# One hybrid decoder layer step on one core: first weight half in front of the tokens, and the first products in front of the mean of squares

## What is computed

```python
def rms_norm(x, g):
    xf = x.astype(jnp.float32)
    y = xf * lax.rsqrt(jnp.mean(xf * xf, -1, keepdims=True) + EPS)
    return (y * g.astype(jnp.float32)).astype(x.dtype)

def mixer_in(x, pos, g_pre, w_in):
    z = rms_norm(x, g_pre) @ w_in
    u = z[..., :CONV_CH] * jax.nn.sigmoid(z[..., CONV_CH:c0])
    ...   # q, k, v and gates are further columns of z
```

## Time and profile before

| | |
|---|---|
| time, median of 3 runs | 779.73 us (779.62 to 781.24) |
| time of the profiled execution | 778.18 us |
| its span in the profile | 775.7 us |
| mean granted clock of PE | 0.988 |
| busy: PE, DVE, ACT, POOL | 745.4, 465.4, 249.2, 316.0 us |

### The profile page before, as it was taken

The page is one execution under the profiler, slowest core; times in us unless marked ns, Lnnn a source line. Parts: engine busy times, 40 slices in busy tenths (PEclk is TensorE's granted clock), DMA queues, the critical chain, the costliest instruction groups (busy, mean ns, idle before and its releaser), DMA issues.

```text
span 775.7 us, 14868 instructions
## 1 busy us (share of the span) xinstructions
PE 745.4 (96%) x6211; PEld 698.6 (90%) x6211; DVE 465.4 (60%) x683; ACT 249.2 (32%) x447; POOL 316.0 (41%) x130
## 2 busy tenths in 40 slices
PE   8999999999998798999999999999999999999993
PEld 7999999987897655589999999999999999999992
DVE  5999978788767477833296333800025767733236
ACT  6422532243556577653343212200002122110021
POOL 1100000023301300002607576876775876776774
PEclk9999999999999799999999999999999999999997
DMA  9532420357624931101314133153223133123103
GB/s 359 181 108 99 138 96 18 133 177 220 229 96 129 288 10 55 56 1 55 109 57 163 55 109 108 56 216 108 63 100 109 56 108 108 58 106 108 55 1 110
DMA packets 25041, 85.50 MB, mean 110 GB/s; under 512 B 7216, under 2 KB 12896, under 8 KB 17760
## 3 DMA queue, kind: packets, MB, share of 16 engines
q1 hardware_dynamic: 17760, 62.13, 24.6%
q0 software_dynamic: 3456, 16.78, 6.6%
q10 hardware_dynamic: 3776, 5.89, 2.0%
HBM read 80.51 MB, written 8.47 MB: 115 GB/s over the span
## 4 chain that ended last, share of the span: by engine, by line
PE 89%; DVE 6%; ACT 3%; issue 1%; DMA 1%; SPq 0%; DVEq 0%; ACTq 0%
PE PA L1527 27%; PE PB L1527 27%; PE PB L1850 5%; PE PB L1538 2%; PE PA L1538 2%; PE PR L1952 2%; PE PR L1702 1%; PE PS L1987 1%; PE PS L1723 1%; PE PB L1978 1%; PE PA L1978 1%; DMA wraw<-wblk_dram 1%; DVE smx L1334 1%; PE PA L1687 1%; PE PR L1629 1%
## 5 line engine op out<-in xcount | busy, mean ns | idle before, releaser
L434 POOL TENSOR_TENSOR wH<-wraw,zero 128x2048 fp32r<-128x2048 f32 x29 | 105.3, 3631 | 110.6 <-PE PB L1527 87.1
L437 POOL TENSOR_TENSOR wL<-wraw,wH 128x2048 fp32r<-128x2048 f32 x29 | 139.5, 4811 | 2.3
L1429 DVE TENSOR_TENSOR hL<-h,hH 128x520 f32 (+1 forms) x32 | 64.6, 2022 | 47.1 <-ACT hH L883 47.1
L881 ACT ACTIVATE h<-rl 128x520 f32<-128x520 f32 x32 | 20.4, 638 | 209.3 <-DVE rl L1424 208.6
L999 DVE SCALAR_TENSOR_TENSOR yC<-uP,vec,yC 128x512 f32<-128x512 f32 (+1 forms) x135 | 84.2, 682 | 0.1
L1527 PE MATMUL PA<-hL,wH 128*128 128x260 f32 x240 | 67.7, 282 | 0.0
L1527 PE MATMUL PB<-hL,wH 128*128 128x260 f32 x240 | 67.7, 282 | 0.0
L1527 PE MATMUL PA<-hH,wL 128*128 128x260 f32 x240 | 67.7, 282 | 0.0
L1527 PE MATMUL PA<-hH,wH 128*128 128x260 f32 x240 | 67.7, 282 | 0.0
L1527 PE MATMUL PB<-hH,wL 128*128 128x260 f32 x240 | 67.7, 282 | 0.0
L1527 PE MATMUL PB<-hH,wH 128*128 128x260 f32 x240 | 67.7, 282 | 0.0
(11 more groups left out here) (515 smaller groups left out, 2317.8 us busy)
## 6 DMA issues: line engine op xcount, KB each, us to landing
wraw<-wblk_dram SPq DMA_DIRECT2D x46, 1024.0 KB, 4.8
xT<-x_fm_dram SPq DMA_DIRECT2D x4, 520.0 KB, 5.0
xT<-x_fm_dram SPq DMA_DIRECT2D x1, 2080.0 KB, 12.6
y_fm_dram<-xT SPq DMA_DIRECT2D x8, 260.0 KB
rkw<-cwk_dram SPq DMA_DIRECT2D x8, 256.0 KB, 2.8
s_win_dram<-cwk_dram ACTq DMA_DIRECT2D x1, 2044.0 KB
s_win_dram<-cwv_dram ACTq DMA_DIRECT2D x1, 2044.0 KB
p_rows_dram<-ktok ACTq DMA_DIRECT2D x4, 256.0 KB, 3.3
```

Source lines behind the costliest of these rows:

```text
L434: pool.tensor_tensor(wH[1 - s][:, :], wraw[s][:, :], zero[:, :].broadcast_to([P, BW]), ALU.add)\
L437: pool.tensor_tensor(wL[1 - s][:, :], wraw[s][:, :], wH[1 - s][:, :].bitcast(F32), ALU.subtract)\
L881: act.activation(h2[c % 2][:, :], rl[c % 2][:, :], ACT.Square).then_inc(s_h2, 1)
L1429: dve.tensor_tensor(lo, h2[c % 2][:, :], hi.bitcast(F32), ALU.subtract).then_inc(s_hl, 1)
```

## The change

SP issues the vectors first, then the first half of the first block (k = 0 to 3) with a semaphore of its own, the first two token tiles, the second half of the block, and then the other token tiles. DVE applies the gains to its four parts ahead of the pair adds. PE makes the first block's products for k = 0 and 1, then the sums of pairs 0 and 1, the products for k = 2, the sums of pairs 2 and 3, and then the products for k = 3 to 7. ACT's list stays as it is: the root still stands ahead of its gains. Nothing else differs; the same instructions run, with one transfer more.

```diff
@@ sync
-            for i in range(4):
+            sp.dma_start(vec[:, :], A["vecs"]).then_inc(s_vec, 16)
+            sp.dma_start(wraw[0][:, 0:BW // 2], A_wblk[B_IN][:, 0:BW // 2]).then_inc(s_w0, 16)
+            load_x(0)
+            sp.dma_start(wraw[0][:, BW // 2:BW], A_wblk[B_IN][:, BW // 2:BW]).then_inc(s_raw[0], 16)
+            for i in range(1, 4):
                 load_x(i)
-            sp.dma_start(vec[:, :], A["vecs"]).then_inc(s_vec, 16)
-            sp.dma_start(wraw[0][:, :], A_wblk[B_IN]).then_inc(s_raw[0], 16)
             sp.dma_start(wraw[1][:, :], A_wblk[B_IN + 1]).then_inc(s_raw[1], 16)
@@ vector
+            dve.wait_ge(s_vec, 16)
+            dve.wait_ge(s_w0, 16)
+            for k in range(4):
+                dve.tensor_scalar(first_w[:, k * 2 * P:(k + 1) * 2 * P], wraw[0][:, k * 2 * P:(k + 1) * 2 * P],
+                                  vec[:, V_GPRE + k:V_GPRE + k + 1], None, ALU.mult).then_inc(s_gwd, 1)
             for k in range(0, KT, 2):
                 dve.wait_ge(s_sq0, k + 2)
                 dve.tensor_tensor(psq[k][:, :], psq[k][:, :], psq[k + 1][:, :], ALU.add).then_inc(s_sqp, 1)
-            dve.wait_ge(s_vec, 16)
-            dve.wait_ge(s_raw[0], 16)
-            for k in range(4):
-                dve.tensor_scalar(first_w[:, k * 2 * P:(k + 1) * 2 * P], wraw[0][:, k * 2 * P:(k + 1) * 2 * P],
-                                  vec[:, V_GPRE + k:V_GPRE + k + 1], None, ALU.mult).then_inc(s_gwd, 1)
             rinv(1, 1)
@@ tensor
-            for k in range(0, KT, 2):
-                pe.wait_ge(s_sqp, k // 2 + 1)
+
+            def mean_pair(p):
+                pe.wait_ge(s_sqp, p + 1)
                 for hf in range(2):
-                    mm = pe.matmul(PB[:, hf, 0:HT], ones[:, 0, :], psq[k][:, hf * HT:(hf + 1) * HT],
-                                   start=(k == 0), stop=(k == KT - 2))
-            mm.then_inc(s_st, 1)
+                    mm = pe.matmul(PB[:, hf, 0:HT], ones[:, 0, :], psq[2 * p][:, hf * HT:(hf + 1) * HT],
+                                   start=(p == 0), stop=(p == KT // 2 - 1))
+                if p == KT // 2 - 1:
+                    mm.then_inc(s_st, 1)
@@ tensor, in the loop over k of the first block's products
                     if k == KT - 1:
                         mm.then_inc(s_grp, 1)
+                for p in {1: (0, 1), 2: (2, 3)}.get(k, ()):
+                    mean_pair(p)
             pe.wait_ge(s_split, SPLITS(B_IN + 1))
             pe.wait_ge(s_std, 1)
             first_groups((B_IN + 1) % 2, 0)
```

More of the change, by code:

```diff
@@ L305, in hymba_step @@
         s_sm = sem("att_small")
+        s_w0 = sem("first_weights_half_loaded")
         s_tv, s_ta, s_tp = sem("tail_dve"), sem("tail_act"), sem("tail_pe")
```

## The result

The changed kernel is slower: 786.26 us median (784.79 to 788.4, 6 runs) against 779.67 us (777.52 to 781.24, 6 runs) for the kernel before in the same session. The ratio is 1.0092, 95% interval 1.0076 to 1.0109, that is +7.2 us (5.9 to 8.5). The forecast was +4.4. The direction and the mechanism were right, the size was too small: the ratio on 779.73 us gives 786.9, just above the range's end of 786.8.

What follows compares the result with a forecast made beforehand. PE, 89% of the chain, was taken to bound the kernel; 2.75 us of later second block plus 1.7 us of low clock made +4.4 us, so 784.1 us, range 781.3 to 786.8.

Steps and rivals of the forecast that it cites:

- the mechanism: At the start: products ahead of pair sums delay the mean's chain, PE idles for the second block's `wL`, the clock falls.
- The idle time: Before the second block: PE done at 24.1 us waits for `wL` until 28.4, some 4.2 us.
- the slack of 1.24 us: Second block's `wL`: the mean's chain could come 1.24 us later before PE, taking the block at 25.67, would wait.
- The 1.6 us to be won on the products: First block on PE: all products through at 24.1 us instead of 25.67, 1.6 us won but inside the idle time.
- the transfers: First loads: half block lands at 4.95 us, tokens 0 and 1 at 6.25, second half at 7.5.
- The fixed part: Transfers at the start: 2.4 us of each transfer's time is fixed, apart from its size.
- right behind its 11 first matmuls: PE's start: products begin at about 6.4 us instead of 11.76, the first matmuls ending at 6.06.
- The second clock fall: PE's clock falls near 28 us in the `wL` wait; 3.4 us of work at half speed loses 1.7 us.
- 4.0 as planned: The mean's chain: `s_st`, which the root follows, comes at 15.55 us instead of 11.53, 4.0 us later.
- The clock stays up: Rival: the stall before the second block is there but the clock doesn't fall; +3.1 us, 782.8 us, chance 0.27.
- The change doesn't do what it says: Rival: half block, tokens and second half interleave, tokens land near 7.5 us; about +5.5 us, 785; no separate chance.
- absorbed: Rival: a later PE wait for a transfer takes up the shift; about 780 us, no change, chance 0.07.

Runs made afterwards that it cites:

- e_contig: The changed kernel with the first block laid out in memory as two halves, each with its 4096-byte rows contiguous; ratio to the kernel before 1.0061.
- e_wlfirst: The changed kernel with VectorE making the second block's `wL` in front of the first tile's normalization instead of the sixth; ratio to the kernel before 1.0114.
- e_warm: The changed kernel with 22 instead of 11 matmuls on the ones matrix at the start; ratio to the kernel before 1.0095.
- e_warmfill: The changed kernel with 22 ones-matrix matmuls at the start and 18 more before the wait for the second block's `wL`; ratio to the kernel before 1.0071.
- e_fit: The changed kernel with three token transfers first, reordered pair sums and earlier `wL`s, three convolution steps put off, halves at the old pitch; ratio to the kernel before 1.0057.
- e_oldloads: The changed kernel with the old order of transfers: four token transfers, vectors, then the block in two halves; ratio to the kernel before 1.0150.
- e_whole: The changed kernel with the first block in one transfer of 8192 bytes a row, right behind the vectors; ratio to the kernel before 1.0093.

## Why the prediction was wrong in size

**Right: the mechanism.** The root behind the products, everything on VectorE behind the root, TensorE idle for the second block's `wL`, and the clock falling in that gap: all are in the chain after. The idle time was predicted as 4.2 us and is 4.07; the slack of 1.24 us as well (the `wL` 6.7 later, TensorE 5.4 later). The 1.6 us to be won on the products were not won in the change: they end at 26.99, 1.3 later than before. In e_contig they end at 24.48, 1.2 earlier, and that vanishes in the idle time of 4.08, as predicted.

**The step that failed: the transfers.** "the half block can't start before 1.3 and lands at 1.3 + 2.4 + 1.25 = 4.95; tokens 0 and 1 at 6.25." They landed at 6.2 and 7.43. I took the half block's 1.25 us from a transfer of whole rows of 8192 bytes. e_contig gives the half block contiguous rows and lands at 5.35 and 6.5, with the root at 15.76 for my 15.55 and the second block at 28.56 for my 28.4: with this one term put right, the sum of the prediction holds to 0.2 us up to the stall. Of the 1.2 us by which the half block was late, 0.85 is what the place of its rows makes (6.2 against 5.35), and 0.4 is there with contiguous rows too. The rate that I used is not wrong for every half row: the second half moved at it. I had bounded the landing by 0.5 us upwards, from the issue alone; the row rate of a form that the trace doesn't show was no part of the bound, and should have been. The fixed part was rather too small than too large: the 2.0 us of the Trainium skill (DMA: Bandwidth & Descriptors, "Anatomy of one DMA"), a section on transfers that the general engine issues, would have put the half block 0.4 us earlier still, and e_contig has it 0.4 later than forecast.

**What hung on it, and was left out: the first clock fall.** I had PE start "right behind its 11 first matmuls, which end at 6.06". They ended at 5.34 in this execution and the tokens came at 7.43; the gap of 2.19 us was followed by a clock of 0.50, and the two first tiles took 5.43 us instead of 3.5, all of it in front of the pair sums. In the root's 2.7 us beyond the forecast these are 1.2 of landing and 1.9 of clock, less 0.4: the 0.1 of waiting for the second pair, and 0.3 of the last pair sum, which took 0.88 right behind other matmuls and not the forecast's 1.15. The gap wasn't all of the landing's making: with first matmuls that end at 6.06 it would have been 1.5. In e_wlfirst a gap of 1.21 went with first products as slow, so how long a gap is needed stays open; that an unbroken PE has none of it is what e_warm and e_warmfill show. I had seen that 2.21 us of waiting at 249.63 left the clock at 1.00 and never asked the question at the start.

**The second clock fall** was forecast at 1.7 us; it took 1.4 in the change (the second block 13.4 us long instead of 11.9), 2.4 in e_contig. Its length is 3.4 us in one run and 6.8 in another, so 1.7 was a middle value of something that moves by itself, and that it came near is in part luck. The second fall, behind 4.07 us, agrees with the Trainium skill (TensorE: Matmul & The Clock Gate, "Why this matters for your kernels"), which warns of idle gaps between bursts of matmuls. The first came behind a gap of 2.19 us, shorter than those it warns of; there the measurement decides.

**The rivals.** "The clock stays up" is what e_warmfill makes: +4.8 with the late landing. "The change doesn't do what it says", with tokens that "land near 7.5", came true for the tokens, by another cause than the interleaving that I named (e_contig has the same order of transfers, and tokens at 6.5), and I had priced it without the first clock fall. Not absorbed: no later wait took up any of the shift.

**The sum with the measured terms.** Root: 4.0 as planned, 1.2 of landing, 1.9 of clock, less 0.4, is 6.7. Less the slack of 1.3 in front of the second block it is 5.4; the second clock fall adds 1.4, and 6.8 is what n = 4 shows. VectorE's own 6.7 less 0.93 would have been 5.8, so the third block's `wL` was no longer waited for. The timed +7.2 (5.9 to 8.5) holds the 6.8.

## What to carry to other kernels

Before work is put in front of a reduction because TensorE "is idle anyway", ask who waits for the reduction's result: here it was the whole list of VectorE, with 1.2 and 0.9 us of slack, and each microsecond beyond them came out at the other end, at whichever `wL` was next. A tensor cut into column halves need not be two transfers of half the time each: here the first half was slow and the second was not, and laying the halves out apart made both fast. Measure the form that you will use. And TensorE's idle gaps can be paid twice when the clock falls in them, at the start of a kernel as well.

## What the runs showed of the hardware

- The first half of the block, rows of 4096 bytes at a pitch of 8192 bytes, moved at 181 to 301 GB/s in the change (3 to 6 us, with the first of it still starting up), at 201 to 219 in e_fit (7 to 9 us) and at 258 to 278 in e_oldloads (8 to 10 us). The same bytes contiguous moved at 381 to 427 in e_contig (4 to 6 us), and whole rows of 8192 at 426 in e_whole (4 to 5 us). The second half, of the same form as the first, moved at 414 in e_oldloads (10 to 11 us). So the form alone doesn't set the rate, and the cause is open. The Trainium skill (DMA: Bandwidth & Descriptors, "Latency and other measured facts") has rates that fall with row pitches of large powers of two, from 512 KiB to 4 MiB; no run here shows those, and this one is at 8 KiB.
- After an idle gap of 2.19 us at the start the granted clock fell to the 1.2 GHz level; after one of 2.2 us at 249 us it fell in some executions of one and the same kernel and not in others. The low stretches lasted from 3.4 to 13.7 us.
- Those moments are a large part of the spread between runs: two executions of the kernel before are the same to 0.3 us up to 250 us, and 3.8 us apart at the end, with two falls of the clock in between that cost 1.67 and 1.6.
